# Two blocks of transformer layers on one Trainium2 core: moving the conditioning's gate work into the FFN, one subtraction a pair later, and one to GpSimd

## The reference

```python
sh_a, sc_a, g_a, sh_f, sc_f, g_f = split(silu(c) @ w_ada + b_ada, 6)   # the conditioning
# for the latent tokens with c, for the context tokens with c_ctx
y = attention(x * (1 + sc_a) + sh_a) @ w_out
x = layer_norm(ALPHA * x + g_a * y)          # layers 1 and 2; layer 0: x + g_a * y, rms norm
f = ffn(x * (1 + sc_f) + sh_f)               # conv_ffn in layers 1, 2; swiglu in layer 0
x = layer_norm(ALPHA * x + g_f * f)
```

## Time and profile before

| | us |
|---|---|
| median of 3 runs (2739.36 to 2744.16) | 2740.14 |
| the profiled execution, its own time | 2734.7 |
| span of its instructions | 2732.9 |
| PE busy in the span | 2437.1 (89%) |
| DVE busy | 1638.0 (60%) |
| ACT busy | 974.2 (36%) |
| POOL busy | 372.1 (14%) |
| DMA, mean | 93 GB/s |

### The profile page before, as it was taken

One profiled execution on the slowest core, in us unless ns is written; L12 is line 12 of the kernel. 1 busy time (PEld: TensorE's weight loads), 2 busy tenths in 40 slices (PEclk: granted clock), 3 DMA queues, 4 the chain that ended last, 5 costly groups with the idle time before them and its releaser, 6 DMA issues.

```text
span 2732.9 us, 33500 instructions
## 1 busy us (share of the span) xinstructions
PE 2437.1 (89%) x13322; PEld 1969.1 (72%) x13322; DVE 1638.0 (60%) x2766; ACT 974.2 (36%) x1766; POOL 372.1 (14%) x359
## 2 busy tenths in 40 slices
PE   5998897999989899888779999999968896999995
PEld 5875566778878777555567888888857675878774
DVE  3539575565665642887768755554564877545355
ACT  2425452422212422666132332332332763424232
POOL 0010102100021000000110212212231001101122
PEclk9999999999999999999889999999988998999998
DMA  6222023744543221000403323331212022222221
GB/s 232 66 74 78 23 63 139 248 144 139 170 136 126 93 75 62 32 28 27 142 16 131 125 81 108 126 110 60 70 55 77 32 78 77 98 89 91 85 85 46
DMA packets 79066, 255.47 MB, mean 93 GB/s; under 512 B 5696, under 2 KB 10432, under 8 KB 70464
## 3 DMA queue, kind: packets, MB, share of 16 engines
q1 hardware_dynamic: 63936, 199.25, 21.4%
q0 software_dynamic: 13680, 49.81, 5.4%
q10 hardware_dynamic: 1296, 4.28, 0.4%
HBM read 243.88 MB, written 9.44 MB: 93 GB/s over the span
## 4 chain that ended last, share of the span: by engine, by line
PE 67%; DVE 12%; ACT 6%; issue 5%; POOL 2%; DMA 1%; DVEq 0%; POOLq 0%; ACTq 0%
PE PS L958 10%; PE PS L960 10%; PE PS L959 10%; PE PS L993 5%; PE PS L994 5%; PE PS L995 4%; PE PS L825 3%; PE PS L728 3%; PE PS L725 3%; PE PS L726 3%; PE PS L838 2%; ACT HT L2133 2%; PE PS L867 2%; DVE SM L1566 2%; DVE ACC L1364 1%
## 5 line engine op out<-in xcount | busy, mean ns | idle before, releaser
L958 PE MATMUL PS<-HH,WH 128*128 128x512 f32 x1056 | 416.5, 394 | 6.4 <-DVE WL L1766 4.8
L959 PE MATMUL PS<-HL,WH 128*128 128x512 f32 x1056 | 414.5, 393 | 0.0
L960 PE MATMUL PS<-HH,WL 128*128 128x512 f32 x1056 | 414.3, 392 | 0.0
L1994 ACT ACTIVATE WH<-STG 128x1024 fp32r<-128x1024 f32 (+1 forms) x204 | 198.9, 1023 | 335.9 <-PE PS L995 256.1
L993 PE MATMUL PS<-WH,AH 128*128 128x512 f32 x616 | 249.5, 405 | 42.3 <-DVE AL L1863 25.0
L1766 DVE TENSOR_TENSOR WL<-STG,WH 128x1024 fp32r<-128x1024 f32 (+1 forms) x204 | 240.0, 1218 | 69.0 <-ACT WH L1994 68.7
L1364 DVE SCALAR_TENSOR_TENSOR ACC<-ADAW,CS,ACC 128x1024 f32<-128x1024 f32 x182 | 246.5, 1393 | 29.1 <-DMA ADAW<-in_w_ada 26.9
L994 PE MATMUL PS<-WL,AH 128*128 128x512 f32 x616 | 246.1, 399 | 0.0
L995 PE MATMUL PS<-WH,AL 128*128 128x512 f32 x616 | 245.4, 398 | 0.0
L958 PEld LDWEIGHTS PS<-HH,WH 128*128 128x128 f32 x1056 | 200.8, 190 | 48.7 <-issue 5.4
L960 PEld LDWEIGHTS PS<-HH,WL 128*128 128x128 f32 x1056 | 200.3, 190 | 42.1
(11 more groups left out here) (204 smaller groups left out, 4394.8 us busy)
## 6 DMA issues: line engine op xcount, KB each, us to landing
STG<-in_w_up SPq DMA_DIRECT2D x66, 1024.0 KB, 6.9
ADAW<-in_w_ada SPq DMA_DIRECT2D x96, 512.0 KB, 4.0
ADAW<-in_w_ada POOLq DMA_DIRECT2D x40, 512.0 KB, 4.1
STG<-in_w_down SPq DMA_DIRECT2D x20, 1024.0 KB, 5.2
STG<-in_w_ffn_out SPq DMA_DIRECT2D x10, 1024.0 KB, 7.4
STG<-in_ev_w_in SPq DMA_DIRECT2D x8, 1024.0 KB, 5.3
spill<-X POOLq DMA_DIRECT2D x14, 512.0 KB, 4.9
STG<-in_w_in SPq DMA_DIRECT2D x6, 1024.0 KB, 5.4
```

The costliest lines, as they stand in the source:

```text
L958: e.matmul(PS[:, b, 0:T], h_, HH[gi][:, c, :], start=first, stop=False)
L959: e.matmul(PS[:, b, 0:T], h_, HL[gi][:, c, :], start=False, stop=False)
L960: return e.matmul(PS[:, b, 0:T], l_, HH[gi][:, c, :], start=False, stop=last)
```

## The change

1. Layer 0's `w_out`: VectorE takes four units of entry 3 ahead of the tiles and two after each tile instead of three after each; GpSimd takes its four loads ahead of its tiles too. What is left is finished after the stage's drain.
2. Layer 1's `w_out`: one unit of entry 10 after each of the first five tiles, on PE, VectorE and GpSimd, instead of three. The rest of it is done in the first FFN entries (2, 3 and 0 units), and entries 11 to 15 follow from the fourth entry on. SP issues no rows in the first two entries.
3. Layer 2's entry 16 moves from `w_out` to the FFN, two units for each entry; its rows are loaded by SP.
4. The low part of an output weight quarter (L1610) is made one pair later than the high part.
5. In layer 1's `w_out` GpSimd makes the low parts of the input tiles (`low`) with a new semaphore `pl_xl`, after it has issued its eight DMAs; its bias adds of the layer norm come one turn later.

```diff
-ADA_LOAD = (1, 2, 3, 10, 16)
+ADA_LOAD = (1, 2, 3, 10)
+def ffn_steps(L, pi):
+    return (2, 3, 0)[pi] if L == 1 and pi < 3 else 2
 # SP, ffn
-            step(bg, 2)
+            step(bg, 0 if L == 1 and pi < 2 else 2)
-        ffn(L, ada(11, 16) if L == 1 else iter(()))
+        ffn(L, ada(11, 16) if L == 1 else ada(16, 17))
 # PE, w_out
-                w.wait_ge(*k.dv_xl((L, tt, c // 4)))
+                w.wait_ge(*(k.pl_xl if L == 1 else k.dv_xl)((L, tt, c // 4)))
-                step(bg, 3)
-        step(bg, 100)
+                step(bg, 3 if L == 0 else int(i < 5))
 # PE and VectorE, ffn, each entry
-            step(bg, 2)
+            step(bg, ffn_steps(L, pi))
 # PE and VectorE, layers 1 and 2
-        w_out(L, ada(10, 11) if L == 1 else ada(16, 17))
+        bg = ada(10, 16) if L == 1 else ada(16, 17)
+        w_out(L, bg if L == 1 else iter(()))
-        ffn(L, ada(11, 16) if L == 1 else iter(()))
+        ffn(L, bg)
 # VectorE, attention
-            if out_split(L, p):
-                out_weights_low(L, 0, *out_split(L, p))
+            if out_split(L, p - 1):
+                out_weights_low(L, 0, *out_split(L, p - 1))
 # VectorE, w_out
-        low(0)
-        low(1)
+        if L != 1:
+            low(0)
+            low(1)
...
+        if L == 0:
+            step(bg, 4)
...
-            if i + 2 < len(WOUT_TT[L]):
+            if L != 1 and i + 2 < len(WOUT_TT[L]):
                 low(i + 2)
...
-            step(bg, 3)
+            step(bg, 2 if L == 0 else int(i < 5))
 # GpSimd, w_out, layers 1 and 2
-            for tt in WOUT_TT[L]:
-                step(blocks, 3)
-                layer_norm("a", L, tt)
+            tts = WOUT_TT[L]
+            def low(i):
+                xh, xl = k.out_parts(L, i)
+                for h in range(2):
+                    x = slice(h * 512, h * 512 + 512)
+                    w.wait_ge(*k.ac_xh((L, tts[i], h)))
+                    e.tensor_tensor(xl[:, x], k.x(tts[i])[:, x], xh[:, x].bitcast(F32),
+                                    ALU.subtract).then_inc(*k.pl_xl.up((L, tts[i], h)))
+            if L == 1:
+                low(0)
+                low(1)
+            for i in range(len(tts)):
+                if L == 1 and i + 2 < len(tts):
+                    low(i + 2)
+                if i:
+                    layer_norm("a", L, tts[i - 1])
+                step(blocks, int(i < 5))
 # GpSimd, w_out, layer 0, ahead of the tiles
+        step(blocks, 4)
 # GpSimd, ffn, in each "up" entry
+                step(blocks)
```

More of the change, by code:

```diff
@@ L258, in __init__ @@
         self.pl_x = sig("pl_x")
+        self.pl_xl = sig("pl_xl")
         self.pl_gate = sig("pl_gate")
@@ L604, in sync_program @@
         project(L)
-        for s in range(2):
-            ada_free[s] = [k.dv_ada((10, 6 + s, 1))]
         if L == 1:
+            for s in range(2):
+                ada_free[s] = [k.dv_ada((10, 6 + s, 1))]
             neighbourhood(0)
@@ L1137, in tensor_program @@
     w_out(0, bg)
+    step(bg, 100)
     e.drain().then_inc(*k.pe_end.up(("wo", 0)))
@@ L1625, in pairs @@
             step(bg, ada_steps(p))
-            if out_split(0, p):
-                out_weights_low(0, 0, *out_split(0, p))
+            if out_split(0, p - 1):
+                out_weights_low(0, 0, *out_split(0, p - 1))
         normal(name, L, n - 1, items[-1]["nk"], 5)
@@ L2538, in w_out, with ffn @@
         spill(LAT[-1])
-    def ffn(L):
+    def ffn(L, blocks):
         F, plan, chunks, groups = k.ff[L], PLAN[L], CHUNKS[L], GROUPS[L]
@@ L2629, in gpsimd_program @@
     e.drain().then_inc(*k.pl_end.up(("wo", 0)))
-    ffn(0)
+    ffn(0, iter(()))
     e.drain().then_inc(*k.pl_end.up(("ff", 0)))
@@ L2646, in gpsimd_program @@
             gate_bias(L, 5, v, [])
-        blocks = row_blocks(10, 11) if L == 1 else row_blocks(16, 17)
+        blocks = row_blocks(10, 11) if L == 1 else iter(())
         step(blocks, 2)
@@ L2651, in gpsimd_program @@
         e.drain().then_inc(*k.pl_end.up(("wo", L)))
-        ffn(L)
+        ffn(L, blocks)
         e.drain().then_inc(*k.pl_end.up(("ff", L)))
```

## The result

The changed kernel takes 2786.15 us (median of 4 runs, 2782.31 to 2793.03) against 2739.75 (4 runs): ratio 1.0169, 95% interval 1.0145 to 1.0192. It is 46 us slower, where 31 us faster was forecast, and lies outside the range. The profiled execution of the kernel after took 2793.0 us, 7 above its runs' median (its span is 2791.0), and that of before was 5 under its own median; so the spans of the two traces stand 58.1 us apart.

What follows compares the result with a forecast made beforehand. PE, busy 89% of the span, was taken as the bound, leaving its stands and low-clock work to gain from. Terms -8.1, -7.8, -11.2 and -4.3 sum to -31.4 us, 2740.1 to 2709; forecast 2702 to 2715, range 2696 to 2724.

Steps and rivals of the forecast that it cites:

- Layer 1's first FFN entries: Layer 1's FFN: PE stands at entry 10's L641, SP's later rows delay no product; +2.5 us (0 to +5).
- Rival C: FFN: gate work not hidden, SP's fetch behind rows waiting for VectorE; layer 2 +24.8 us, total 2733; chance 0.07.
- Both signs: Marks of a wrong forecast: PE idling anew in layer 2's up entries, or pairs with a quarter keeping 6.5 us.
- Low parts a pair later: Attention, all layers: VectorE's waits for ScalarE before L1610 go; -8.1 us (0 to -12), 3.8 of it in layer 0.
- Layer 0's `w_out`: Layer 0's output projection: VectorE starts the last tile at 470.5 instead of 478.3, tail hangs on spills; -7.8 us.
- Layer 2's `w_out`: Layer 2's output projection without units: transposes start 13.1 us sooner, part paid back in the FFN; sum -11.2 us (-8 to -12).
- Layer 1's `w_out`: Layer 1's output projection: fewer units, GpSimd's low halves collide with VectorE, turns of 14.0 us; -6.8 us (-16.9 to +1).
- Rival A: Layer 1's w_out: collisions stay small, turns follow PE, 10.1 us more gained, total 2699; chance 0.15.
- Rival D: Layer 1's w_out: GpSimd's low halves come onto PE's path in all six tiles; slower, 2754 at 5 us each; chance 0.03.

Runs made afterwards that it cites:

- e1: The changed kernel with SP issuing no conditioning rows in the first three entries of layer 1's FFN instead of two: 2699.16 us, ratio to before 0.9866.
- e6: e4 with the low part of an output weight quarter back in the same pair as its high part, all layers: 2705.03 us, ratio to before 0.9878.
- e7: e4 with layer 0's output projection as before, no units ahead of the tiles and three after each: 2702.15 us, ratio to before 0.9868.
- e8: e4 with entry 16 back in layer 2's output projection, three units a tile, loaded by GpSimd: 2702.77 us, ratio to before 0.987.
- e4: e1 with the low parts of layer 1's input tiles made by VectorE again instead of GpSimd: 2690.89 us, ratio to before 0.9829.
- e10: e4 with the norm's bias adds in layer 1's output projection moved from GpSimd to VectorE: 2686.04 us, ratio to before 0.9814.
- e11: e10 plus, in layer 1's w_out, two of entry 10's units ahead of the tiles and one after each of the first three: 2682.8 us, 0.9798.
- e2: Kernel before, PE and VectorE taking no conditioning units in layer 1's first FFN entry, two in each later; SP's rows as before: 2843.23 us, ratio 1.0389.
- e12: e11 with a third unit ahead of layer 1's tiles and one less in the second FFN entry: 2683.87 us, ratio to before 0.9802.

## Why the prediction was wrong

**The step that failed** is this sentence of "Layer 1's first FFN entries": "SP's rows start later there, no product waits for them." It looked at the rows and not at what is queued behind them. The term was given as +2.5 (0 to +5), though 17.5 less 14.6 is 2.9; it measured +91.8, of which 3.35 are the term as meant (`e1`) and the rest, 88.4, is SP's order. In the changed kernel SP starts entry 11 one FFN entry before VectorE does, so its wait for a sum is one for the same entry, and the weight fetch behind that wait, without which the entry after next can't begin on time, goes out when PE is at the end of its work.

**Rival C** had the right mechanism, "SP's fetch stands behind rows that wait for VectorE", with 0.07, and in the wrong layer: it was priced for layer 2's four entries at 6.2 each, where nothing of it appeared, and against it stood layer 0's FFN, which has SP and VectorE in step, as layer 1's no longer had. Ten stands of 6.5 us in the mean, close to its price of 6.2, are 64.8 us, and PE is busy 23.6 us longer than in `e1`, with a granted clock of 0.92 against 0.98: together the 88.4. Counting units would have shown it: by the diff SP begins entry 11 in the third FFN entry and VectorE in the fourth; before, both began in the first. Both signs that the prediction named for being wrong (new idle time in layer 2's up entries, pairs that keep 6.5 us) stayed away; none was set where the error lay.

**The other steps**, by the stage windows above and the experiments that undo each:
- *Low parts a pair later*, -8.1: right in sum (-10.4; -8.1 by `e6`), but not by layer. In layer 0 it was to bring 3.8 and brought 0.1 in this trace, 1.3 by `e6`. The four quarter pairs fell, as said, but to 5.90 us and not to the 5.55 of pairs with L1364, from 6.52. Layer 1 gave 6.1 (2.5 by `e6`), layer 2 4.2 (4.3 by `e6`). Layer 1's size is uncertain: its attention takes 209.1 to 210.5 us in all eleven kernels with the later low parts, 213.0 in `e6`, and 215.2 before. Why the last two differ is open.
- *Layer 0's `w_out`*, -7.8: exact, and 7.8 by `e7`. The last tile starts at 470.34, the forecast was 470.5; the tail hung on the spills, as said.
- *Layer 2's `w_out`*, -11.2: right (-11.8; 12.6 by `e8`). The price in the FFN was 1.1, and PE's idle time there is the same (23.9 and 24.0).
- *Layer 1's `w_out`*, -6.8: right (-6.2), but with some luck, since two errors of opposite sign stand in it. PE's stand was 4.36 for the 5.4 forecast. A turn took 14.71 for 14.0: the low halves cost VectorE 2.66 a tile, not 1.9, the bias adds 2.16, as forecast. Turns without low halves took 12.0 for 12.1.
- *Rival A* (no collisions) is refuted by `e4` and `e10`. *Rival D* (GpSimd's halves on PE's path in all tiles) didn't occur, but its sign for this part was right: the part costs time (`e4`, 8.3 us), by way of VectorE.

The Trainium skill, SBUF — State Buffer, section SBUF: two separate sides, says that the port pair of VectorE and GpSimd is an exclusive lock, held for a whole instruction. The traces agree in the size: 3.35 us is 0.69 and the whole 2.54 us of the two halves, with 0.12 over. The Trainium skill also says there that whoever starts first gets the pair. The rows don't show that: VectorE's add starts at 1327.26, GpSimd's two halves at 1327.52 (its times are rough), and still the add ended behind both.

The forecast's fault was thus one term of the sum, and a range that came from the terms that were seen. Twelve experiments give the parts their places; without the slip in SP's count the change is 1.3% faster than before, without GpSimd's low parts too 1.7%, and with the order of `e11` 2.0%.

## What to carry to other kernels

When background work starts later on one engine, count its units on every engine that shares the generator, and ask of each in-order queue what stands behind the wait: a fetch queued behind a wait for this entry's result can be an entry late. The lag between the issuer and the user of a buffer had slack on one side only here: one entry more cost nothing, one less 87 us (`e1`) and 106 (`e2`). So if in doubt, hold the issuer back rather than let it run ahead. Before moving a two-input operation to GpSimd, look at what VectorE does beside it: here 1.29 us saved cost 2.66, since VectorE had a two-input SBUF operation there.

## What the runs showed of the hardware

- VectorE's adds with both inputs in SBUF are held up for about as long as GpSimd runs such an operation beside them: 0.69 us became 3.35 beside two halves of 1.27 us, and the 2.48 of two sums became 4.64 beside a bias add of 2.33 that itself took 3.38.
- A row of 512 KB issued by GpSimd at the start of layer 1's `w_out` took up to 12.4 us to land, elsewhere 4.2: the six loads of the old x and SP's weights were under way at once, and the row above from `e12` is what came of it. The windows of `e12` in that stretch, with the DMA share of 0.93 next to last:

```profile
1284.00:1304.00 20.00, 20.00 (x88) 16.26 (x87) 9.69 (x11) 4.51 (x6) 3.04 (x6) 1.00 0.93 356
```

The Trainium skill, DMA: Bandwidth & Descriptors, section Issuing engines are not separate DMA queues, says that loads of all engines run on the same 16 DMA engines. The trace agrees: in this window the packets of the queue that GpSimd feeds took 67.4% of the 16 engines' time, those of the hardware queue with SP's loads 25.0%.
- Layer 0's FFN, which none of the changes touches, took between 398.2 us (`e2`, `e11`) and 405.0 (`e6`) in the fourteen profiled executions, by where PE fell to its low clock. `e2` and the kernel before are the same program up to layer 1's FFN, and yet layer 0's FFN took 398.2 and 401.4 us in them, and layer 1's projections, next behind it, 180.4 and 177.7. The mean granted clock goes the other way, 0.98 and 0.97 in the FFN, 0.96 and 0.97 in the projections: work at the low clock had moved from the one stage into the other. So a few us in one of these stages don't show by themselves what a change did. Why one execution gets the one length and another the other stays open.
